# Moving the sample attention's score steps within the mixing stage of a two-layer decoder step

## The reference

```python
x = x + 0.5 * swiglu(rmsnorm(x, g_ffn1), f1_in, f1_out)
z = rmsnorm(x, g_mix) @ w_in       # pooling input u, q/k/v of 6 attention heads, q/k/v/gate of 6 retention heads
#  A: causal pooling over windows 2, 4, 8, 16, a map per group, a scale
#  B: softmax attention: blocks of 256 keys, the best 3 past blocks and the own one, ALiBi
#  C: retention with a decay per head, normalised per head, gated with silu
x = x + concat(A, B, C) @ w_out
x = x + 0.5 * swiglu(rmsnorm(x, g_ffn2), f2_in, f2_out)
```

## Time and profile before

| | us |
|---|---|
| median of 3 runs | 1453.36 |
| lowest, highest | 1450.92, 1453.76 |
| the profiled execution | 1445.9 |
| its span, first to last instruction | 1443.9 |
| mean granted PE clock of the span | 0.974 of full speed |

### The profile page before, as it was taken

How to read it: one execution, slowest core, us unless ns; L and a number is a source line. 1 busy time by engine, 2 the same in 40 slices (tenths; PEclk the granted TensorE clock), 3 DMA queues, 4 the chain that set the end, 5 groups by cost and what they waited for, 6 DMA issues and landing times.

```text
span 1443.9 us, 28417 instructions
## 1 busy us (share of the span) xinstructions
PE 1360.1 (94%) x11165; PEld 1306.2 (90%) x11165; DVE 812.1 (56%) x870; ACT 650.0 (45%) x715; POOL 216.7 (15%) x343
## 2 busy tenths in 40 slices
PE   6999999899877999999999999989997789999998
PEld 4999999899656899999999999989984579999998
DVE  4655545477673665554455555456867546555454
ACT  4655533334223565553355554432434245555433
POOL 3000001370334100000100000034313611000001
PEclk9999999999988999999999999999999899999998
...
GB/s 207 150 145 145 143 160 180 209 166 115 219 179 277 118 145 146 151 152 144 152 142 156 152 145 135 158 236 142 208 110 221 258 153 146 145 145 145 142 153 121
...
## 3 DMA queue, kind: packets, MB, share of 16 engines
...
...
q10 hardware_dynamic: 120, 0.03, 0.0%
...
## 4 chain that ended last, share of the span: by engine, by line
PE 84%; issue 7%; DVE 5%; DVEq 1%; POOLq 1%; DMA 1%; ACT 1%; POOL 0%; SPq 0%; ACTq 0%
PE ps L1235 21%; PE ps L1237 21%; PE ps L1236 21%; PE ps L1317 4%; PE ps L1319 4%; PE ps L1318 4%; PE ps L1457 2%; DVE kbuf L990 1%; PE ps L1495 1%; PE ps L1402 1%; DVEq L1165 1%; PE ps L1630 1%; DVE h_lo L851 0%; DVE w_lo L844 0%; DMA x_tok<-in_x_sample 0%
## 5 line engine op out<-in xcount | busy, mean ns | idle before, releaser
L587 ACT ACTIVATE w_hi<-w_raw 128x2048 fp32r<-128x2048 f32 x170 | 325.6, 1915 | 554.6 <-PE ps L1237 427.3
L844 DVE TENSOR_TENSOR w_lo<-w_raw,w_hi 128x2048 fp32r<-128x2048 f32 x170 | 391.4, 2303 | 210.4 <-ACT w_hi L587 207.7
L1235 PE MATMUL ps<-h_hi,w_hi 128*128 128x320 f32 x768 | 241.0, 314 | 9.5 <-DVE w_lo L844 3.5
L1236 PE MATMUL ps<-h_lo,w_hi 128*128 128x320 f32 x768 | 239.7, 312 | 0.0
L1237 PE MATMUL ps<-h_hi,w_lo 128*128 128x320 f32 x768 | 239.5, 312 | 0.0
L1235 PE MATMUL ps<-g_hi,w_hi 128*128 128x320 f32 x704 | 218.4, 310 | 1.2 <-DVE g_lo L851 1.2
L1237 PE MATMUL ps<-g_hi,w_lo 128*128 128x320 f32 x704 | 217.7, 309 | 0.0
L1236 PE MATMUL ps<-g_lo,w_hi 128*128 128x320 f32 x704 | 217.7, 309 | 0.0
L1236 PE MATMUL ps<-act_lo,w_hi 128*128 128x320 f32 x704 | 217.5, 309 | 0.0
L1235 PE MATMUL ps<-act_hi,w_hi 128*128 128x320 f32 x704 | 217.5, 309 | 0.0
L1237 PE MATMUL ps<-act_hi,w_lo 128*128 128x320 f32 x704 | 217.5, 309 | 0.0
...
## 6 DMA issues: line engine op xcount, KB each, us to landing
w_raw<-in_ffn_w_in SPq DMA_DIRECT2D x90, 1024.0 KB, 5.1
...
kbuf<-in_cache_k SPq DMA_DIRECT2D x128, 192.0 KB, 3.3
w_raw<-in_w_in SPq DMA_DIRECT2D x22, 1024.0 KB, 5.7
w_raw<-in_ffn_w_out SPq DMA_DIRECT2D x16, 1024.0 KB, 5.0
...
w_raw<-in_w_out SPq DMA_DIRECT2D x8, 1024.0 KB, 7.5
...
```

Of the source, the lines that this page charges most:

```text
L587: act.activation(w_hi[:, slot, :], w_raw[:, slot, :], ACT.Copy).then_inc(hi_done, 1)
L844: dve.tensor_tensor(w_lo[:, slot, :], w_raw[:, slot, :], w_hi[:, slot, :].bitcast(F32), ALU.subtract).then_inc(split_done, 1)
L1235: pe.matmul(out, w_hi[:, slot, w], hi[:, k, :], start=(k == 0), stop=False)
L1236: pe.matmul(out, w_hi[:, slot, w], lo[:, k, :], start=False, stop=False)
```

## The change

The step `sample_scores(0)` moves from after chunk 5 to before it, `sample_scores(1)` from after chunk 9 to before it, `sample_scores(2)` some steps earlier, behind `att_out(2)`, and `sample_scores(3)` from after `mean_squares` to between `ret_out(2)` and `smp_state(2)`. `scores(f)`, `transpose_p` and `past_states` move about one gap later. The key loads, `turn_k`, `soft_in`, `soft_bias`, `exps` and `qprep` move along with them; in SP's list `next_k(1, *)` now stands before `mix_load(7)`, and `next_k(2, *)` before `mix_load(10)`. The fourth pair's scores get a tile of their own, `sp_d`, in slot 0 of `w_lo`, so that `mix_lo(12)` waits for `transpose_probs(3)`. `out_part(0)` moves behind `smp_out(2)` and `transpose_out(2)`. Some transposes use other PSUM banks. No arithmetic changes. The changed lines, with a line around them (indentation reduced):

```diff
...
 sp_c = at("sp_c", [96, PAST_LEN + SMP], F32, w_lo_at, 8)
-sp = [sp_a, sp_b, sp_c, sp_a]
+sp_d = at("sp_d", [96, PAST_LEN + SMP], F32, w_lo_at, 0)
+sp = [sp_a, sp_b, sp_c, sp_d]
 v_c = at("v_c", [P, PAGES, HDIM], F32, arena_at, 0)
...
         load_k(0, 1, half)
-    for c in range(3, 8):
+    for c in range(3, 7):
         mix_load(c)
+    next_k(1, 0)
+    next_k(1, 1)
+    mix_load(7)
     sp_e.wait_ge(u_out, 2 * L + 2)
...
     mix_load(8)
-    next_k(1, 0)
     sp_e.wait_ge(ka_out, 3 * L + 2)
     store_kv(0, "k", ka_tok, None, stored_k)
-    next_k(1, 1)
     mix_load(9)
+    next_k(2, 0)
+    next_k(2, 1)
+    mix_load(10)
     sp_e.wait_ge(va_out, 3 * L + 2)
     store_kv(0, "v", va_tok, None, stored_va)
-    mix_load(10)
     mix_load(11)
-    next_k(2, 0)
-    next_k(2, 1)
     sp_e.wait_ge(ka_out, 3 * L + 3)
...
         src_p, src_s = dst_p, dst_s
-        if n == 1:
+        if n == 0:
             pool.wait_ge(q_own, L + 1)
...
     load_v_all(1)
+    wait_apart(pool, own_done, L * 4 + 3)
+    qprep(L, 3)
+    pool.drain()
     wait_apart(pool, oa_done, 3 * L + 3)
...
     spread_v(3)
-    wait_apart(pool, own_done, L * 4 + 3)
-    qprep(L, 3)
-    pool.drain()
     spread_v(4)
...
         else:
-            act.activation(v_own[:, :], ps[0:SMP, 6, 0:HDIM], ACT.Copy).then_inc(va_out, 1)
+            act.activation(v_own[:, :], ps[0:SMP, 3, 0:HDIM], ACT.Copy).then_inc(va_out, 1)
...
         act.wait_ge(pt_done, H * L + (h + 1))
-        act.activation(pt_p[:, h % 2, :], ps[:, 2 if h % 2 else 6, 0:384], ACT.Copy).then_inc(pt_evac, 1)
+        act.activation(pt_p[:, h % 2, :], ps[:, (6, 2, 6, 2, 6, 7)[h], 0:384], ACT.Copy).then_inc(pt_evac, 1)
...
     act.activation(q_rep[:].rearrange("p g f t -> p g (f t)"), ps[:, 4:8, 0:192], ACT.Copy).then_inc(qr_ok, 1)
+    act.wait_ge(evac_done, L * G_ALL + (GROUPS0 + G_MIX + 4))
+    act.activation(k_own[:], z[:, ZKA:ZKA + 3, SEQ:], ACT.Copy).then_inc(kown_ok, 1)
     mix_hi(6)
-    act.activation(k_own[:], z[:, ZKA:ZKA + 3, SEQ:], ACT.Copy).then_inc(kown_ok, 1)
     u_tokens()
...
     ka_tokens(1)
+    exps(0)
     exp(0)
...
     va_tokens(0)
+    mix_hi(9)
+    va_tokens(1)
     probs_out(0)
...
     exp(3)
-    mix_hi(9)
-    va_tokens(1)
-    exps(0)
     mix_hi(10)
     att_evac(0)
+    exps(1)
+    mix_hi(11)
+    ka_tokens(2)
     probs_out(2)
...
     exp(5)
-    mix_hi(11)
-    ka_tokens(2)
+    att_evac(1)
     va_tokens(2)
-    att_evac(1)
     probs_out(4)
     probs_out(5)
-    exps(1)
     act.wait_ge(stored_va, 16 * (L + 1))
...
     act.wait_ge(stored_u, 32 * (L + 1))
+    exps(2)
     for f in range(3):
...
         root_o(f)
-    exps(2)
     probs_evac(0)
-    for f in range(3):
-        or_high(f)
+    exps(3)
     out_evac(0, 0)
...
     probs_evac(1)
+    for f in range(3):
+        or_high(f)
     y_high(0)
-    exps(3)
-    mix_hi(12)
     out_evac(1, 0)
...
     y_high(1)
+    mix_hi(12)
     out_evac(2, 0)
...
         evac_first(c)
+        turn_k(0, 0, c)
         evac_last(c)
...
     evac_first(2)
-    turn_k(0, 0, 0)
+    turn_k(0, 1, 0)
     evac_last(2)
     mix_lo(4)
+    dve.drain()
+    dve.tensor_copy(q_smp[:], z[:, ZQA:ZQA + 3, SEQ:]).then_inc(q_own, 1)
     dve.wait_ge(loaded, 16 * len(C))
...
     evac_first(3)
-    turn_k(0, 0, 1)
+    turn_k(0, 1, 1)
     evac_last(3)
     mix_lo(5)
-    dve.drain()
-    dve.tensor_copy(q_smp[:], z[:, ZQA:ZQA + 3, SEQ:]).then_inc(q_own, 1)
     evac_first(4)
-    turn_k(0, 1, 0)
     evac_last(4)
+    mix_lo(6)
+    soft_in(0)
+    evac_first(5)
+    soft_bias(0)
+    evac_last(5)
+    mix_lo(7)
     smax(0)
...
     smax(1)
-    mix_lo(6)
-    evac_first(5)
-    turn_k(0, 1, 1)
-    evac_last(5)
-    mix_lo(7)
+    evac_first(6)
+    turn_k(1, 0, 0)
+    evac_last(6)
+    mix_lo(8)
     normalise(0)
     normalise(1)
-    soft_in(0)
-    evac_first(6)
-    soft_bias(0)
-    evac_last(6)
+    turn_k(1, 0, 1)
+    evac_first(7)
+    turn_k(1, 1, 0)
+    evac_last(7)
+    mix_lo(9)
+    turn_k(1, 1, 1)
     smax(2)
...
     smax(3)
-    mix_lo(8)
-    evac_first(7)
+    evac_first(8)
...
     ins.then_inc(q_dec_ok, 1)
-    evac_last(7)
+    evac_last(8)
+    mix_lo(10)
     normalise(2)
     normalise(3)
-    mix_lo(9)
     soft_sum(0)
-    turn_k(1, 0, 0)
-    evac_first(8)
-    turn_k(1, 0, 1)
-    evac_last(8)
+    dve.wait_ge(pool_d, L + 1)
+    soft_in(1)
+    evac_first(9)
+    soft_bias(1)
+    evac_last(9)
+    mix_lo(11)
     smax(4)
...
     smax(5)
-    mix_lo(10)
-    turn_k(1, 1, 0)
-    evac_first(9)
-    turn_k(1, 1, 1)
-    evac_last(9)
+    evac_first(10)
+    turn_k(2, 0, 0)
+    evac_last(10)
+    turn_k(2, 0, 1)
     dve.wait_ge(past_done, L + 1)
...
     ins.then_inc(past_ok, 1)
-    mix_lo(11)
     normalise(4)
     normalise(5)
-    dve.wait_ge(pool_d, L + 1)
-    dve.wait_ge(stored_k, 32 * L + 16)
-    soft_in(1)
-    evac_first(10)
-    soft_bias(1)
-    evac_last(10)
     evac_last(11)
+    turn_k(2, 1, 0)
+    turn_k(2, 1, 1)
+    soft_sum(1)
+    dve.wait_ge(chunk_used, L * C_ALL + (C_MIX + 14))
+    soft_in(2)
     dve.wait_ge(stored_k, 32 * (L + 1))
...
     k_tokens(0)
-    turn_k(2, 0, 0)
     k_tokens(1)
-    turn_k(2, 0, 1)
     dve.wait_ge(att_high, L + 1)
...
     k_tokens(2)
-    turn_k(2, 1, 0)
-    turn_k(2, 1, 1)
     decay_mask(1)
+    soft_bias(2)
+    turn_k(3, 0, 0)
     for t in range(2):
...
     decay_mask(3)
+    turn_k(3, 0, 1)
     gate(0)
-    soft_in(2)
+    decay_mask(4)
+    turn_k(3, 1, 0)
     new_state(0)
-    decay_mask(4)
+    decay_mask(5)
+    turn_k(3, 1, 1)
     gate(1)
     new_state(1)
-    decay_mask(5)
     gate(2)
+    soft_in(3)
     new_state(2)
-    soft_sum(1)
-    soft_bias(2)
+    soft_sum(2)
+    soft_bias(3)
...
-    for half in range(2):
-        turn_k(3, 0, half)
-    or_norm(0)
-    for half in range(2):
-        turn_k(3, 1, half)
-    soft_in(3)
-    soft_sum(2)
-    soft_bias(3)
-    or_norm(1)
-    or_norm(2)
+    for f in range(3):
+        or_norm(f)
     y_rest(0)
...
         or_lo(f)
+    y_rest(1)
+    dve.wait_ge(pt2_done, NB * L + 8)
     mix_lo(12)
-    y_rest(1)
     soft_sum(3)
     y_rest(2)
-    dve.wait_ge(pt2_done, NB * L + 6)
     mix_lo(13)
...
         pe.wait_ge(p_norm, H * L + (h + 1))
-        if h % 2:
-            pe.wait_ge(sm_in, L * 4 + 1 + h // 4)
-        elif h == 0:
+        if h == 0:
             pe.wait_ge(u_out, 2 * L + 2)
-        elif h == 4:
-            pe.wait_ge(va_out, 3 * L + 3)
+        elif h == 3:
+            pe.wait_ge(sm_in, L * 4 + 2)
+        elif h == 5:
+            pe.wait_ge(oa_out, 3 * L + 2)
         if h >= 2:
...
         for n, c in enumerate((256, 0, 128)):
-            ins = pe.transpose(ps[:, 2 if s else 6, P * n:P * n + P], s_p[:, s, c:c + P], ident[:])
+            ins = pe.transpose(ps[:, (6, 2, 6, 2, 6, 7)[h], P * n:P * n + P], s_p[:, s, c:c + P], ident[:])
         ins.then_inc(pt_done, 1)
...
     def past_states():
-        pe.wait_ge(sm_in, L * 4 + 1)
+        wait_apart(pe, sm_in, L * 4 + 2)
         wait_apart(pe, q_dec_ok, L + 1)
...
     u_tokens()
-    scores(0)
     tokens(ZKA, 0, 7).then_inc(ka_tr, 1)
+    pe.wait_ge(kown_ok, L + 1)
+    sample_scores(0)
     mix(5)
...
     tokens(ZKA, 1, 7).then_inc(ka_tr, 1)
-    pe.wait_ge(kown_ok, L + 1)
-    pe.wait_ge(s_max, H * L + 2)
-    sample_scores(0)
+    wait_apart(pe, sm_in, L * 4 + 1)
+    scores(0)
     mix(6)
...
     tokens(ZVA, 0, 7).then_inc(va_tr, 1)
-    transpose_p(0)
-    transpose_p(1)
-    scores(1)
     mix(7)
...
     tokens(ZVA, 1, 7).then_inc(va_tr, 1)
+    transpose_p(0)
+    transpose_p(1)
+    wait_apart(pe, s_max, H * L + 2)
+    scores(1)
     mix(8)
...
     att_out(0)
-    transpose_p(2)
-    transpose_p(3)
-    wait_apart(pe, s_max, H * L + 4)
-    scores(2)
-    past_states()
+    pe.wait_ge(s_max, H * L + 4)
+    sample_scores(1)
     mix(9)
...
     tokens(ZKA, 2, 7).then_inc(ka_tr, 1)
-    wait_apart(pe, pt_evac, H * L + 4)
-    tokens(ZVA, 2, 6).then_inc(va_tr, 1)
-    pe.wait_ge(s_max, H * L + 6)
-    pe.wait_ge(past_ok, L + 1)
-    sample_scores(1)
+    transpose_p(2)
+    transpose_p(3)
+    scores(2)
+    past_states()
     mix(10)
...
     att_out(1)
+    wait_apart(pe, past_ok, L + 1)
+    tokens(ZVA, 2, 3).then_inc(va_tr, 1)
+    mix(11)
+
     transpose_p(4)
     transpose_p(5)
-    mix(11)
-
     mixed(12)
...
     tokens(ZKR, 0, 0).then_inc(kr_tr, 1)
-    wait_apart(pe, oa_out, 3 * L + 2)
     att_out(2)
     tokens(ZVR, 0, 6).then_inc(vr_tr, 1)
+    pe.wait_ge(s_max, H * L + 6)
+    pe.wait_ge(va_out, 3 * L + 3)
+    sample_scores(2)
     wait_apart(pe, kr_out, 3 * L + 1)
...
     ret_scores(1)
-    sample_scores(2)
...
     ret_out(2)
+    sample_scores(3)
     smp_state(2)
-    wait_apart(pe, sm_in, L * 4 + 3)
+    wait_apart(pe, sm_in, L * 4 + 4)
     mean_squares()
...
     transpose_probs(0)
-    wait_apart(pe, o_std, 3 * L + 3)
-    sample_scores(3)
     wait_apart(pe, st_prm, L + 1)
...
     transpose_out(1)
```

(10 more changed lines are left out.)

## The result

The changed kernel takes 1536.57 us (median of 4 runs, 1534.95 to 1539.55) against 1452.14 for the kernel before (4 runs): a ratio of 1.0592, 95% interval 1.0570 to 1.0614. It is slower by 84 us where I had forecast 56, and it lies above my range of 1480 to 1532. The profiled execution has a span of 1534.5 us against 1443.9, 90.6 more.

The account below looks back on a forecast made before the run. TensorE bounds the kernel, busy 1360.1 of 1443.9 us. Per layer 8.1 + 2.0 + 16.9 + 2.5 + 2.2 - 1.7 - 2.0 = 28.0, 56.0 for both: 1453.4 + 56.0, say 1509 us; range 1480 to 1532.

Parts of the forecast that it names:

- Part 1: Pair 0's scores before chunk 5: nothing gained or lost, PE at 323.45 after chunk 6 and tokens(ZVA, 0).
- Part 2: Chunk 7's load behind pair 1's keys: issued at 316.8, landed at 323.6, PE starts chunk 7 at 331.6.
- stall 1: PE's wait before chunk 7 in each layer: 8.1 us, with bounds 7.0 to 10.4.
- clock term: Lower granted clock after the wait before chunk 7: 2.0 us a layer, 1.3 to 2.7.
- Part 3: Chunk 10's load behind pair 2's keys: 16.9 us wait a layer, 2.5 clock at past_states, 2.2 for o_past, 1.7 removed.
- t: Start of sample_scores(1), now before chunk 9; about 351 us in layer 0.
- Part 4: Second stretch, up to FFN 2: PE waits of 26.6 us but less low clock; 2.0 gained a layer (6.0 gained to 2.0 lost).
- A: Rival: the weights for chunks 7 and 10 land in time and the kernel is faster, 1446 us; chance 0.04.
- B: Rival: the keys' 10.4 us issue is busy-DMA back-pressure and shrinks; 8.8 us less a layer, 1492; chance 0.05.
- C: Rival: only the wait around chunk 10 exists, not chunk 7's; 10.1 us less a layer, 1489; chance 0.05.
- stall 2: PE's waits between chunks 9 and 10 in each layer: 16.9 us, with bounds 15.8 to 19.2.
- D: Rival: the second stretch gives its 25 us of waits back almost wholly; 20 more a layer, 1470; chance 0.03.

Follow-up runs that it names:

- e2: Changed kernel with only chunk 7's weight load moved back ahead of pair 1's key loads: 1517.5 us, 1.0477 of the kernel before.
- e7: Changed kernel with chunk 7's and 10's loads ahead of the keys, and pair 2's softmax and pair 3's turn_k behind the retention's start: 1461.7 us.
- e10: e7 with POOL's spread_v ahead of issuing the V pages and DVE's o_past copy ahead of evac_last(10): 1444.8 us, 0.9977 of the kernel before.
- e13: Changed kernel, weights still behind the keys, with e10's other edits (softmax and turn_k later, spread_v and o_past earlier): 1507.2 us, ratio 1.0404.
- e8: Changed kernel with chunk 7's and 10's loads ahead of the keys, plus 28 unread filler matmuls behind sample_scores(2): 1472.6 us, ratio 1.0150.
- e12: Changed kernel with the 16 key loads each of pairs 1 and 2 carrying half the bytes: 1527.1 us, 1.0529 of the kernel before.
- e9: Changed kernel with chunk 7's and 10's loads ahead of the keys, and past_states' tiny matmuls mixed into chunk 10: 1476.7 us, ratio 1.0182.
- e11: e10 with past_states' tiny matmuls mixed into chunk 10: 1446.9 us, 0.9996 of the kernel before.

## Why the prediction was off, by its own steps

**Part 1 held.** PE was done with chunk 6 at 324.0; the forecast of 323.45 has the 0.3 us of `tokens(ZVA, 0)` in it, so PE was 0.9 late.

**Part 2 held, stall 1.** Issue of chunk 7 at 317.30 (316.8), landed 324.34 (323.6), PE's start 332.48 (331.6). The wait is 2.74 + 5.19 = 7.9 us (8.1); the first piece comes because `ka_tokens(1)` stands behind `mix_hi(7)` on ACT, which I had not named. Removing it by the load's place (e2) brings 8.6 us a layer. Its clock term was 2.0, and chunk 7 took 9.79 against the 7.3 of the kernel before: 2.5.

**Part 3 held in its wait, and was short in its clock.** t was 352.07. The weights went out at t + 15.0 (t + 13.7, the keys taking 11.49 instead of 10.4), landed at t + 23.0 (20.5), and the waits are 12.86 + 1.84 + 3.14 = 17.8 us (16.9). Chunk 10 started at t + 44.9, not t + 37.1. Of the 7.8 us between, 0.9 is the larger wait and 0.5 that chunk 9 ended at t + 12.4, not t + 11.9; the rest is work at half clock. `past_states` took 10.6 us where it had 6.2 in the earlier trace rows: 4.4, for which I took 2.5 with a bound of 5.0: this term was mis-sized. Its three groups of 14 after the change:

```profile
386.76 3.17 PE L1403 MATMUL ps<-q_dec,s 128*128 128x16 f32 x14
...
390.18 3.17 PE L1403 MATMUL ps<-q_dec,s 128*128 128x16 f32 x14
...
393.60 3.17 PE L1403 MATMUL ps<-q_dec,s 128*128 128x16 f32 x14
```

The tokens, transposes and `scores(2)` between the waits took 1.9 more, and chunk 11, behind the wait for `o_past` (2.17, forecast 2.2), 1.3 more. I had priced neither. In sum the clock of the first stretch was 11.0 a layer, not 4.5. That low clock behind `past_states` merely moves from chunk 9 to chunk 10 was right: 9.8 us there, 9.94 here.

**Part 4 failed, in its clock: it is the one part whose stretch fell outside my bounds.** I wrote that in return for the 26.6 us of waits "the long idle time goes, and with it part of the low clock", took a gain of 2.0, and bounded the loss at 2.0. The layer lost 7.8 there. The waits came out smaller than I had walked them, 22.3 us in all, 2.8 fewer than before. The first of them, 4.4 by my walk and 4.33 in the trace, and the one ahead of `ret_out(0)`, 3.3 by my walk and 2.07 in the trace, were in my list; I had priced them as idle time and nothing else. In the kernel before, the retention's matmuls up to `ret_out(2)` ran at full clock, and here most of them run at half behind these two waits. The same 81 matmuls, from `ret_scores(2)` to the start of `ret_out(2)`, before:

```profile
394.40:404.90 10.50, 9.01 (x81) 1.00 0.99 340
```

and after:

```profile
435.70:453.30 17.60, 15.36 (x81) 0.60 0.38 133
```

In between, the clock came back once, for about 3 us, and fell again at the second wait:

```profile
436.00:438.00 2.00, 2.00 (x9) 0.75 1.05 394
438.00:440.00 2.00, 0.58 (x5) 1.00 1.03 369
440.00:442.00 2.00, 1.35 (x14) 0.61 0.95 311
```

After that it was back only at `sample_scores(3)`, some 30 us after its first fall. That the waits were the cause, e7, e10 and e13 show by removing them: e13's second stretch is 12.7 us shorter than after's, and 9.7 of these are busy time (75.3 instead of 85.0). e8 shows the limit: part of that slow work is hidden, and holding the clock without removing DVE's delay brings some 0.7 us a layer, if anything.

**The account.** The first stretch is 7.1 us a layer over the forecast and the second 9.8, together 16.9, and 33.8 for both layers: from 56.0 to 89.8 of the 90.6 us of span. Had the second stretch brought its 2.0, the sum would have been 70 and the time inside the range; it would have been inside too without the 7.1 of the first, but those lay within my bounds and the second stretch did not. That the clock terms were read from chunk 9 and from the 9.8 us behind the wait of 7.4 is how the mistake was made; and chunk 9 was no case of a wait, since PE was busy for 10.95 of 11.00 us there. Above all, I asked what a stall does to the next chunk, not to all the work until the clock is back.

**The rivals.** A (weights in time) is refuted by the ACT rows, B (back-pressure set by the bytes) by e12, C (stall 2 alone) by PE's rows. D, that the second stretch gives back its waits, is false for this kernel; but e10 shows that some of them were to be had: 18.4 us of idle time instead of 25.0, by another order on DVE and POOL.

**What stays open.** What drops the clock within `past_states` while PE is busy, and why with mixing it fell in one layer of e9 and of e11 and not in the other. And whether the waits that e10 has left in its second stretch (the V page 2.5 us, `w_lo` of chunk 12 2.6) can go as well was not tried.
